# One gather of 8 KB rows, holding an expert's u row and v row side by side, in place of two gathers of 4 KB rows

## The reference, cut to what matters

```python
def peer_ffn(x, w_query, sub_keys, u_table, v_table):
    ...                       # scores against 2 x 128 keys per head, top 16 of the sums
    expert = idx1 * PEER_KEYS + idx2
    gate = jax.nn.softmax(c_top, axis=-1)
    def block(args):
        xb, eb, gb = args
        u = u_table[eb]
        hid = jax.nn.gelu(jnp.einsum('td,thkd->thk', xb, u)) * gb
        return jnp.einsum('thk,thkd->td', hid, v_table[eb])
```

## Time and profile before

| | |
|---|---|
| median of three runs | 3848.17 us |
| profiled execution: its own time | 3848.43 us |
| its span | 3846.7 us |
| mean granted TensorE clock | 0.959 |
| busy: PE / DVE / ACT / POOL | 91% / 75% / 26% / 37% |
| bytes moved | 829.65 MB, of which 537.01 MB on the queue of POOL |

### The profile page before, as it was taken

The page is one execution under the profiler, slowest core; times in us unless marked ns, Lnnn a source line. Parts: engine busy times, 40 slices in busy tenths (PEclk is TensorE's granted clock), DMA queues, the critical chain, the costliest instruction groups (busy, mean ns, idle before and its releaser), DMA issues.

```text
span 3846.7 us, 40107 instructions
## 1 busy us (share of the span) xinstructions
PE 3519.2 (91%) x11785; PEld 2016.6 (52%) x11785; DVE 2879.8 (75%) x6784; ACT 995.0 (26%) x2460; POOL 1427.0 (37%) x1232
## 2 busy tenths in 40 slices
PE   7999969999988999557899999999999999999997
PEld 4666647777764665355344434444444444444443
DVE  2466757777771699895878887878788877887887
ACT  3233334444442222232111111112121111111212
POOL 1000000000001477101555555555555555555564
PEclk9999989999979999789999999999999999999999
DMA  3101020001003333136999999999999999999997
GB/s 105 34 28 33 1 110 22 27 27 33 22 1 134 84 56 75 21 129 260 356 367 366 349 344 361 356 338 356 366 366 367 337 373 374 344 343 371 361 367 264
DMA packets 320576, 829.65 MB, mean 216 GB/s; under 512 B 41360, under 2 KB 153104, under 8 KB 310544
## 3 DMA queue, kind: packets, MB, share of 16 engines
q0 software_dynamic: 165888, 537.01, 39.0%
q1 hardware_dynamic: 78640, 227.97, 15.7%
q10 hardware_dynamic: 75872, 62.66, 5.0%
HBM read 789.73 MB, written 37.81 MB: 215 GB/s over the span
## 4 chain that ended last, share of the span: by engine, by line
PE 38%; DMA 11%; DVE 6%; issue 2%; ACT 0%; POOL 0%; DVEq 0%; SPq 0%; ACTq 0%; POOLq 0%
PE peer_ps_o L1713 21%; PE peer_ps_d L1699 13%; DMA peer_mt<-sel 8%; DMA route_ut<-in_u_cols 3%; PE peer_ps_q L1641 3%; DVE peer_mt L1872 1%; PE peer_ps_o L1680 1%; DVE Y L1908 1%; DVE peer_mt L1868 1%; DVE peer_ur L1897 1%; DVE route_hit L1083 0%; DVE peer_chosen L1085 0%; DVE route_hit L1081 0%; PE peer_ps_s L1651 0%; DMA sel<-peer_ur 0%
## 5 line engine op out<-in xcount | busy, mean ns | idle before, releaser
L1699 PE MATMUL peer_ps_d<-hnT,route_ut 128*128 128x512 f32 x2048 | 912.0, 602 | 53.6 <-DMA route_ut<-in_u_cols 51.7
L1609 POOL DMA_INDIRECT peer_ur<-in_u_rows,peer_index x512 | 595.4, 1163 | 937.6 <-DVE peer_ur L1897 604.6
L1699 PEld LDWEIGHTS peer_ps_d<-hnT,route_ut 128*128 128x128 f32 x2048 | 387.9, 192 | 558.2 <-issue 455.0
L1908 DVE SCALAR_TENSOR_TENSOR Y<-peer_vr,peer_hid,Y 128x1024 f32<-128x1024 f32 x512 | 657.2, 1284 | 8.5 <-DMA peer_vr<-in_v_rows,peer_index 8.4
L1897 DVE SCALAR_TENSOR_TENSOR peer_ur<-peer_ur,Y 128x1024 f32<-128x1024 f32 x512 | 626.7, 1224 | 30.8 <-DMA peer_ur<-in_u_rows,peer_index 30.8
L1616 POOL DMA_INDIRECT peer_vr<-in_v_rows,peer_index x512 | 559.3, 1092 | 164.3 <-issue 154.8
L1713 PE MATMUL peer_ps_o<-hnT,Y 128*128 128x512 f32 x1024 | 473.1, 603 | 55.8 <-DVE Y L1884 51.3
L1713 PE MATMUL peer_ps_o<-peer_va,Y 128*128 128x512 f32 x1024 | 474.1, 607 | 0.0
L1713 PEld LDWEIGHTS peer_ps_o<-hnT,Y 128*128 128x128 f32 x1024 | 195.0, 192 | 306.5 <-issue 243.0
L1713 PEld LDWEIGHTS peer_ps_o<-peer_va,Y 128*128 128x128 f32 x1024 | 200.7, 196 | 256.4 <-issue 255.9
L1884 DVE TENSOR_TENSOR Y<-Y,peer_mt 128x512 f32<-128x512 f32 x128 | 89.0, 695 | 317.8 <-ACT Y L1766 177.3
(11 more groups left out here) (272 smaller groups left out, 4714.5 us busy)
## 6 DMA issues: line engine op xcount, KB each, us to landing
route_ut<-in_u_cols SPq DMA_DIRECT2D x128, 512.0 KB
peer_va<-in_v_rows SPq DMA_DIRECT2D x16, 2048.0 KB
hnT<-in_v_rows SPq DMA_DIRECT2D x16, 2048.0 KB
peer_mt<-sel ACTq DMA_DIRECT2D x64, 512.0 KB
route_wk<-in_w_route ACTq DMA_DIRECT2D x14, 1024.0 KB
hnT<-in_w_route SPq DMA_DIRECT2D x9, 1024.0 KB
route_wk<-in_w_route SPq DMA_DIRECT2D x9, 1024.0 KB
w_group<-in_w_ssd SPq DMA_DIRECT2D x16, 512.0 KB, 4.1
```

Source lines behind the costliest of these rows:

```text
L1609: pool.indirect_dma_start(ur[:, r % RING, :], None, u_rows, bass.IndirectOffsetOnAxis(ap=index[:, r // TOPK % 4, r % TOPK:r % TOPK + 1], a ...
L1699: mm = nc.tensor.matmul(ps_d[:, e % 2, :], ut[:, e % 2, k, :], xT[:, k, :], start=(k == 0), stop=(k == KT - 1))
L1908: nc.vector.scalar_tensor_tensor(out=hb, in0=vr[:, s, :], scalar=hid[:, c:c + 1], in1=hb, op0=ALU.mult, op1=ALU.add).then_inc(comb_done, 1)
```

## The change

The two tables are laid side by side in DRAM: row i of the new table is row i of u followed by row i of v, 8 KB. One ring `uv` of five slots of 8 KB takes the place of the two rings (the same bytes). One indirect DMA per row brings both halves, and it waits for `combine(r-5)`. The order on VectorE becomes `dense(s-1)`, `dot(2s)`, `combine(2s-1)`, `dot(2s+1)`, `combine(2s)`: the addition follows its dot by one row instead of two. `hidden` runs once per row instead of once per pair, on single columns. `v_rows` stays as an input for the dense way.

```diff
@@ -1485,8 +1485,7 @@
         def psum(name, shape):
             return ctx.enter_context(nc.psum_tensor("peer_" + name, shape, F32))
 
-        ur = sb("ur", [P, RING, D])
-        vr = sb("vr", [P, RING, D])
+        uv = sb("uv", [P, RING, 2 * D])
         va = sb("va", [P, GE // 2, D])
         mt = sb("mt", [P, 2, SEQ])
         fw = sb("fw", [P, D])
...
@@ -1514,7 +1513,8 @@
         hot_a = [mflat[:, i * 512:(i + 1) * 512].rearrange("p (q c) -> p q c", q=4) for i in range(2)]
         hot_b = [mflat[:, 1024 + i * 512:1024 + (i + 1) * 512].rearrange("p (q c) -> p q c", q=4) for i in range(2)]
         Q = KEYS // 2 * SELB // 4
-        stage = [va[:], vb, Y[:, 0:4, D:MIX], ur[:, 0:4, :]]
+        stage = [va[:], vb, Y[:, 0:4, D:MIX],
+                 uv[:, 0:2, :].rearrange("p a (b d) -> p (a b) d", d=D)]
 
         wq = wk[:, 0:WQ].rearrange("p (k c) -> p k c", k=KT)
         wkeys = wk[:, WQ:WK].rearrange("p (a c) -> p a c", a=2)
...
@@ -1603,32 +1603,14 @@
 
         @block.gpsimd
         def _(pool):
-            def u_row(r):
-                pool.wait_ge(R.routed, DU + r // TOPK + 1)
-                need(pool, dot_done, r - RING + 1)
-                pool.indirect_dma_start(ur[:, r % RING, :], None, u_rows,
+            pool.wait_ge(sel_out[3], sel_stores(3))
+            for r in range(ROWS):
+                if r % TOPK == 0:
+                    pool.wait_ge(R.routed, DU + r // TOPK + 1)
+                need(pool, comb_done, r - RING + 1)
+                pool.indirect_dma_start(uv[:, r % RING, :], None, uv_rows,
                                         bass.IndirectOffsetOnAxis(ap=index[:, r // TOPK % 4, r % TOPK:r % TOPK + 1], axis=0)
-                                        ).then_inc(got_u[r % RING], 16)
-
-            def v_row(r):
-                pool.wait_ge(R.routed, DU + r // TOPK + 1)
-                need(pool, comb_done, r - RING + 1)
-                pool.indirect_dma_start(vr[:, r % RING, :], None, v_rows,
-                                        bass.IndirectOffsetOnAxis(ap=index[:, r // TOPK % 4, r % TOPK:r % TOPK + 1], axis=0)
-                                        ).then_inc(got_v[r % RING], 16)
-
-            pool.wait_ge(sel_out[3], sel_stores(3))
-            for r in range(RING):
-                u_row(r)
-            for r in range(RING):
-                v_row(r)
-            for p in range(PAIRS):
-                for r in (2 * p + RING, 2 * p + 1 + RING):
-                    if r < ROWS:
-                        u_row(r)
-                for r in (2 * p - 2 + RING, 2 * p - 1 + RING):
-                    if RING <= r < ROWS:
-                        v_row(r)
+                                        ).then_inc(got[r % RING], 16)
 
         @block.tensor
         def _(pe):
...
@@ -1765,17 +1747,16 @@
                     act.wait_ge(sel_out[2], sel_stores(2))
                 nc.scalar.activation(ht(e), ps_d[:, e % 2, :], ACT.Gelu).then_inc(gelu_done, 1)
 
-            def hidden(p):
-                m, c = p // UNIT, 2 * (p % 4)
-                act.wait_ge(dot_done, 2 * p + 2)
-                act.wait_ge(R.gated, DU + m + 1)
-                need(act, comb_done, 2 * (p - 3))
-                nc.scalar.activation(act_out[:, c:c + 2], dots[:, c:c + 2], ACT.Gelu).then_inc(activated, 1)
-                act.wait_ge(activated, p + 1)
-                for j in range(2):
-                    k = 2 * (p % UNIT) + j
-                    nc.scalar.activation(hid[:, c + j:c + j + 1], act_out[:, c + j:c + j + 1], ACT.Copy,
-                                         scale=gate[:, m % 4, k:k + 1]).then_inc(hid_done, 1)
+            def hidden(r):
+                n, c = r // TOPK, r % 8
+                act.wait_ge(dot_done, r + 1)
+                if r % TOPK == 0:
+                    act.wait_ge(R.gated, DU + n + 1)
+                need(act, comb_done, r - 7)
+                nc.scalar.activation(act_out[:, c:c + 1], dots[:, c:c + 1], ACT.Gelu).then_inc(activated, 1)
+                act.wait_ge(activated, r + 1)
+                nc.scalar.activation(hid[:, c:c + 1], act_out[:, c:c + 1], ACT.Copy,
+                                     scale=gate[:, n % 4, r % TOPK:r % TOPK + 1]).then_inc(hid_done, 1)
 
             def load_sel(r):
                 if r < 2:
...
@@ -1823,7 +1804,8 @@
                     query_out(n // 2)
                 if s < GE:
                     gelu(g * GE + s)
-                hidden(slot)
+                hidden(2 * slot)
+                hidden(2 * slot + 1)
                 if n < UNITS and n % 2 == 0 and sl == 2:
                     score_out(n // 2)
                 if n + 2 < UNITS and n % 2 == 0 and sl == 3:
...
@@ -1892,20 +1874,18 @@
 
             def dot(r):
                 b, s, c = row_block(r), r % RING, r % 8
-                dve.wait_ge(got_u[s], 16 * (r // RING + 1))
-                need(dve, hid_done, r - 6 if r % 2 == 0 else 0)
-                nc.vector.scalar_tensor_tensor(out=ur[:, s, :], in0=ur[:, s, :], scalar=1.0, in1=Y[:, b, D:MIX],
+                dve.wait_ge(got[s], 16 * (r // RING + 1))
+                need(dve, hid_done, r - 7)
+                nc.vector.scalar_tensor_tensor(out=uv[:, s, 0:D], in0=uv[:, s, 0:D], scalar=1.0, in1=Y[:, b, D:MIX],
                                                op0=ALU.mult, op1=ALU.mult,
                                                accum_out=dots[:, c:c + 1]).then_inc(dot_done, 1)
 
             def combine(r):
                 b, s, c = row_block(r), r % RING, r % 8
-                dve.wait_ge(got_v[s], 16 * (r // RING + 1))
-                if r % 2 == 0:
-                    dve.wait_ge(hid_done, r + 2)
+                dve.wait_ge(hid_done, r + 1)
                 need(dve, comb_done, r)
                 hb = Y[:, b, 0:D]
-                nc.vector.scalar_tensor_tensor(out=hb, in0=vr[:, s, :], scalar=hid[:, c:c + 1], in1=hb,
+                nc.vector.scalar_tensor_tensor(out=hb, in0=uv[:, s, D:2 * D], scalar=hid[:, c:c + 1], in1=hb,
                                                op0=ALU.mult, op1=ALU.add).then_inc(comb_done, 1)
 
             def mean(f):
...
@@ -1947,8 +1927,8 @@
                 for j in range(2):
                     if slot < PAIRS:
                         dot(2 * slot + j)
-                    if slot > 0:
-                        combine(2 * slot - 2 + j)
+                    if 0 < 2 * slot + j <= ROWS:
+                        combine(2 * slot + j - 1)
                 if n < UNITS and sl == 3:
                     route_keys(nc, dve, own, R, n)
                 if n < UNITS and sl == 5:
...
@@ -2026,7 +2006,7 @@
         "w_route": np.concatenate([first("w_query").reshape(KT, P, PH, 2 * P).transpose(2, 1, 0, 3).reshape(PH, P, -1),
                                    first("sub_keys").transpose(0, 3, 1, 2).reshape(PH, P, 2 * KEYS)], 2),
         "u_cols": first("u_table").reshape(KEYS, KEYS, KT, P).transpose(1, 3, 2, 0),
-        "u_rows": first("u_table"),
+        "uv_rows": np.concatenate([first("u_table"), first("v_table")], 1),
         "v_rows": first("v_table"),
         "fin_w": np.broadcast_to(np.asarray(inputs["ln_final_w"]), (P, D)),
     }
```

More of the change, by code:

```diff
@@ L1470, in _, with peer @@
             gate_of(DU - 1)
-def peer(nc, w_route, u_cols, u_rows, v_rows, fin_w, sel, C, Y, hnT, R, out):
+def peer(nc, w_route, u_cols, uv_rows, v_rows, fin_w, sel, C, Y, hnT, R, out):
     with ExitStack() as ctx:
@@ L1547, in peer @@
                                                       sem("o_added"))
-        got_u, got_v = [sem(f"got_u{i}") for i in range(RING)], [sem(f"got_v{i}") for i in range(RING)]
+        got = [sem(f"got{i}") for i in range(RING)]
         dot_done, activated, hid_done, comb_done = sem("dot_done"), sem("activated"), sem("hid_done"), sem("comb_done")
@@ L1969, in _, with block_program @@
                 norm(f)
-def block_program(nc, x, ln_w, w_ssd, par, w_hg, lb_logits, w_out, mix_w, ffn_w, w_route, u_cols, u_rows, v_rows,
+def block_program(nc, x, ln_w, w_ssd, par, w_hg, lb_logits, w_out, mix_w, ffn_w, w_route, u_cols, uv_rows, v_rows,
                   fin_w, sel, out):
@@ L1989, in block_program @@
         mix_out(nc, x, w_out, mix_w, ffn_w, w_route, sel, sel_zeroed, C, Y, osq, ysq, hnT, R)
-        peer(nc, w_route, u_cols, u_rows, v_rows, fin_w, sel, C, Y, hnT, R, out)
+        peer(nc, w_route, u_cols, uv_rows, v_rows, fin_w, sel, C, Y, hnT, R, out)
 def laid_out(inputs):
```

## The result

The changed kernel takes 3855.72 us (median of 18 runs, 3838.65 to 3871.31); the kernel before, run beside it, 3841.84 us (18 runs, 3828.48 to 3851.04). The ratio is 1.0033, interval 1.0018 to 1.0048: slower by 0.33%, some 13 us. The forecast stood 0.6% over its own base and 30 us over this one. The direction was right and the time within the range, but the forecast was more than double the measured rise (30 us against 14 over the same base), and the parts, as the experiments show, were not those of the forecast: two of them failed, in opposite directions, so the right direction was luck.

A forecast was written before the change was run, and what follows sets the result against it. The late `mt` load, sharing full DMA engines with gathers in dense slots, was taken to bound the kernel. Terms +19 (`mt` groups), +6 less 2 (other groups), +5 clock, -1.3 tail gave +26, cut to +24: 3872 us, range 3822 to 3908.

The forecast's parts named there:

- Longer packets against the direct loads: On the DMA queues, 8 KB gathers delay `mt` by 0.5 us a group, and `ut` by 1.5 us in four groups.
- Fewer, longer packets: On the DMA engines, 8 KB gathers cost 6% less, saving 0.9 us on the chain while the critical `mt` load runs.
- Rival A: Faster: the dense half shrinks by all 16 rows' packet saving, 2.8 us a group, 43 us, to 3805 us; chance 0.27.
- `dot` and `combine` one row apart: On VectorE, `combine` waits for its weight, so the slot 4 `mt` load is issued 2.0 us later in twelve groups.
- One ring: Gathers asked for later, once `combine` frees the row, still fit: 0, at most 3 us a group in output slots.
- Clock: TensorE's clock drops after longer waits for `dense`: 1.65 us once more in a quarter of twelve groups, +5 us.
- POOL and ScalarE: 512 fewer gathers issued on POOL and 256 more Gelus on ScalarE: 0 us on the path.
- B: No change: the late `mt` issue is hidden behind the `wk` load in its queue, 3849 us; chance 0.21.
- C: Clearly slower: gathers are served whole before `mt` in every group, 30 us on top, 3902 us; chance 0.12.
- the tail: After the last matmul, one `combine` remains instead of two: -1.3 us.

The follow-up runs named there:

- `mt` early: ScalarE issues the `mt` load right behind `gelu`, ahead of both `hidden`: 1.0012 in the changed kernel, 0.9914 in that with two 4 KB gathers a row.
- Routing in the gap: Routing put before a slot's last `combine`: 0.986 on the kernel before with new order, 1.0028 on the changed kernel, 0.993 on that with 4 KB gathers.
- a wait added to POOL: POOL holds slot 5's gathers until the slot 4 `mt` load lands: 0.9883 on the kernel before with new order, 1.0041 on one ring with 4 KB.

## Why the prediction was wrong in size, and right in direction by luck

Two steps failed, and their errors nearly cancel: the new order, priced at +24 us, measured -35, and the packets, priced at +12 against the direct loads and -13 for their saving, measured +41.

*Longer packets against the direct loads*: this step failed. It saw the turns by packet in the earlier trace rows, took 0.5 us on `mt`, and let the `ut` loads count "only in the four groups outside" the `mt` chain, 6 us in all. Measured, the packets cost 1.07% (41 us), and TensorE's waits for `ut` rose from 35.6 to 77.8 us with them. The mistake was to hold the chain of the trace before fixed. TensorE's waits for `ut` already stood beside those for `dense`, in the same half of nearly every group; once the `mt` load was relieved, `ut` was the last in most groups (the chain of ten of groups 1 to 15 has no `mt` load in it), and what was added to it counted there. The turns themselves were read generously: the shares of the earlier trace rows stand 3.1 to 1, not 4 to 1. By the rule of the Trainium skill's page "DMA: Bandwidth & Descriptors", section "Queues, rings and completion order", an engine drains a packet of one queue before it turns to the next. The page counts such a packet as some 9 to 17 descriptors, so it does not say that one gathered row is one turn. The trace agrees in kind: with 8 KB gathers the landing of `ut` went from 7.2 to 7.9 us and that of the second v load from 16.7 to 19.6. That turns by packet are the mechanism is argued from this, not shown by itself.

*Fewer, longer packets*: the saving of 6% measured 2.7%, against the same ring and order with 4 KB gathers (4.5% against the kernel before). The 0.9 us a group that it was to give the chain does not show; 8 KB against 4 KB was never faster by more than the intervals. Rival A falls with it. The page "Perfetto Trace Analysis" of the Trainium skill, section "DMA Optimizations", says that batching small transfers into larger ones can improve throughput a great deal, with 2 KB into 4 or 8 KB as its example. From 4 to 8 KB this case shows 2.7% less engine time for the same bytes, and a slower kernel.

*`dot` and `combine` one row apart*: this step failed as well. The working of the issue was right, 10.11 us against 10.25 (and a mean of 1.9 us later against 2.0), and its sign in the sum was wrong: 12 x 2.0 = +24 us, where the order alone gained 0.9%, 35 us. The step took the load's duration as given and made every microsecond of a late issue one of time. Issued later, the load took 19.26 us in place of 23.44. No run shows that the late issue costs anything: `mt` early gained 0.2% and 0.1%, within the intervals. Routing in the gap gained 0.5% on two rings, but there the load took longer by as much as it was issued sooner, and on one ring the same edit gained nothing (1.0028 against 1.0033, 0.993 against 0.9926). What the order gains by is known in part. VectorE holding its routing back gives 0.5% in the kernel before; the order without that hold (routing in the gap) gives 1.4%, so it is not the whole, and the rest stays open: u slots are freed and gathers asked for at other times as well.

*One ring*: taken as 0, between 0 and 3 us a group. In the change itself that holds (0.16%, within the intervals). *Clock*: the forecast gave 5 us to a lower clock. The mean granted clock is 0.963 against 0.959, so nothing was lost. With TensorE's waits for `dense` halved, 37.2 to 17.3 us, the mean granted clock of the output half was below 1.00 in one of groups 1 to 15, where it was in nine; that of the dense half, where TensorE now waits for `ut`, was below it in ten, where it was in six. *POOL and ScalarE*: 0, as said.

*The rivals.* B said that the late issue costs nothing, which no run contradicts; its reason, that the load stands behind `wk` in its queue, was not tested, and its time, 3849, rests on packets that cost nothing either. C had the right resource and the wrong load: the wait from the issue of `mt` to `dense(6)` was not over 25 us but 19.26, at most 23.6 in groups 1 to 15, and `ut` was what TensorE waited for. The forecast's sum was +24 for the order, +12 minus 13 for the packets (0.5 and 1.5 us a group against 0.9 and 2 in all), +5 for the clock, -1 for the tail, cut to +24. What was measured is -35 for the order, +6 for the ring (not told from nothing) and +41 for the packets: +12. These parts hold in this sequence only: the ring without the order costs 1.73%.

## What to carry to other kernels

When a change relieves the load that closes the chain, price the rest against the next latest load, not against the old chain: here `mt` gave up 90 us of waits and the time went up. Where bulk gathers nobody waits for share DMA engines with small loads somebody does, longer packets in the bulk can cost more than their lower price per byte returns, and holding some bulk back at the right moment gained 0.3% here. A load that is issued later does not land later by as much: what it meets on the engines changes too. A ring that holds two things until both are used cost nothing here until something else asked for its slack, so try such edits on the version with separate rings first.

## What the runs showed that was not expected

A wait added to an engine made the kernel faster (0.9953, VectorE holding routing back), and a wait added to POOL seems to as well (0.9883 against 0.991), while the same POOL wait with one ring cost 1.15% (1.0041 against 0.9926). A gather of 8 KB rows costs POOL 1.32 us where one of 4 KB costs 1.09 to 1.16, far from double. The DMA queue of the gathers took 2.7% less time for the same bytes in packets of twice the length, and the half of the group that it fills still became longer, while the other half became shorter by nearly as much (60.6 to 63.4 and 59.6 to 56.9 us).
